# The stick-breaking values' projection computed token-major, with the activations stationary

## What is computed

```python
h = rms_norm(x, norm_mix_g[l])
proj = h @ w_in[l]
hq, hf, hi, hg, su, sq, sk, sv, gates = jnp.split(proj, split_at, axis=-1)
o_a = hgrn2_mixer(hq, hf, hi, hg, lb_all[l], hg_norm_g[l])
o_b = s5_mixer(su, ...)
o_c = stick_breaking_mixer(sq, sk, sv, sb_q_g[l], sb_k_g[l])
gate = jax.nn.sigmoid(gates)
merged = sum of gate_b * (o_b @ w_branch[b]) over the three branches
x = x + merged @ w_out[l]
x = x + gated_mlp(rms_norm(x))       # w_up, causal conv of width 3, silu, w_down
```

## Time and profile before

| | us |
|---|---|
| runs shown: median (lowest, highest) | 1436.39 (1435.6, 1438.55) |
| the profiled execution's own time | 1439.06 |
| its span, first to last instruction | 1437.3 |

### The profile page before, as it was taken

The page is one execution under the profiler, slowest core; times in us unless marked ns, Lnnn a source line. Parts: engine busy times, 40 slices in busy tenths (PEclk is TensorE's granted clock), DMA queues, the critical chain, the costliest instruction groups (busy, mean ns, idle before and its releaser), DMA issues.

```text
span 1437.3 us, 26837 instructions
## 1 busy us (share of the span) xinstructions
PE 1413.6 (98%) x9368; PEld 1294.8 (90%) x9368; DVE 1047.8 (73%) x1406; ACT 762.2 (53%) x1059; POOL 152.3 (11%) x195
## 2 busy tenths in 40 slices
PE   8979999999999999999999999999999999999999
PEld 7869998989999999988888888888888888888887
DVE  7897888688788757777687777777777776545443
ACT  6564678944433455454565555555555554344342
POOL 3210000000000002322111111111111110000000
PEclk9999999999999999999999999999999999999999
DMA  7544454445555556666656566656555666666663
GB/s 265 165 147 153 141 176 156 140 144 176 178 173 174 179 168 232 199 196 190 190 177 201 181 193 187 196 179 192 189 191 186 192 188 183 199 198 196 195 203 111
DMA packets 74346, 261.58 MB, mean 182 GB/s; under 512 B 8560, under 2 KB 9104, under 8 KB 74160
## 3 DMA queue, kind: packets, MB, share of 16 engines
q1 hardware_dynamic: 73152, 256.41, 56.6%
q0 software_dynamic: 992, 4.37, 0.9%
q10 hardware_dynamic: 144, 0.01, 0.0%
HBM read 258.66 MB, written 2.10 MB: 181 GB/s over the span
## 4 chain that ended last, share of the span: by engine, by line
PE 84%; DVE 7%; issue 3%; ACT 3%; POOL 1%; DMA 1%; POOLq 0%; SPq 0%; DVEq 0%; ACTq 0%
PE bank L325 38%; PE bank L339 22%; PE bank L327 20%; PE pair L371 3%; DVE w_lo L945 2%; ACT w_hi L642 1%; POOL merged L1496 1%; DMA raw<-w_br 1%; DVE tmp L953 1%; POOL merged L1498 1%; DVE a_in L1110 1%; DVE x_first L1106 0%; DVE tmp L960 0%; ACT tmp L652 0%; ACT a_raw L784 0%
## 5 line engine op out<-in xcount | busy, mean ns | idle before, releaser
L945 DVE TENSOR_TENSOR w_lo<-raw,w_hi 128x1024 fp32r<-128x1024 f32 (+1 forms) x499 | 590.9, 1193 | 323.2 <-ACT w_hi L642 318.7
L642 ACT ACTIVATE w_hi<-raw 128x1024 fp32r<-128x1024 f32 (+1 forms) x499 | 511.3, 1030 | 436.5 <-PE bank L327 221.4
L325 PE MATMUL bank<-h,w_hi 128*128 128x512 f32 x1408 | 488.4, 390 | 0.0
L327 PE MATMUL bank<-h,w_lo 128*128 128x256 f32 x1408 | 397.1, 282 | 0.0
L339 PE MATMUL bank<-a_in,w_hi 128*128 128x256 f32 x2048 | 364.7, 281 | 0.0
L339 PEld LDWEIGHTS bank<-a_in,w_hi 128*128 128x128 f32 x2048 | 314.2, 189 | 4.6 <-issue 4.6
L325 PEld LDWEIGHTS bank<-h,w_hi 128*128 128x128 f32 x1408 | 264.4, 188 | 55.4
L339 PE MATMUL bank<-a_in,w_lo 128*128 128x256 f32 x1024 | 286.9, 280 | 0.0
L327 PEld LDWEIGHTS bank<-h,w_lo 128*128 128x128 f32 x1408 | 266.1, 189 | 0.0
L325 PE MATMUL bank<-act,w_hi 128*128 128x512 f32 x704 | 244.1, 390 | 0.0
L327 PE MATMUL bank<-act,w_lo 128*128 128x256 f32 x704 | 198.5, 282 | 0.0
(11 more groups left out here) (188 smaller groups left out, 1299.9 us busy)
## 6 DMA issues: line engine op xcount, KB each, us to landing
raw<-w_up SPq DMA_DIRECT2D x176, 512.0 KB, 3.8
raw<-w_in SPq DMA_DIRECT2D x160, 512.0 KB, 4.2
raw<-w_down SPq DMA_DIRECT2D x80, 512.0 KB, 4.4
raw<-w_out SPq DMA_DIRECT2D x32, 512.0 KB, 4.2
raw<-w_br SPq DMA_DIRECT2D x16, 512.0 KB, 3.6
raw<-w_br SPq DMA_DIRECT2D x16, 256.0 KB, 3.3
raw<-w_down SPq DMA_DIRECT2D x16, 256.0 KB, 2.7
x_first<-xT SPq DMA_DIRECT2D x4, 512.0 KB, 7.2
```

The lines of the kernel that those rows point to most:

```text
L325: pe.matmul(bank[b][:, :], w[:, k * P:(k + 1) * P], a.rearrange("p a t -> p (a t)"), start=first and n == 0, stop=False, skip_group_check= ...
L327: mm = pe.matmul(bank[b][:, 0:SEQ], l[:, k * P:(k + 1) * P], a[:, 0, :], start=False, stop=last and n == len(blocks) - 1, skip_group_check ...
L642: act_e.activation(w_hi[s][:, 0:blocks * P], raw[s][:, 0:blocks * P], ACT.Copy).then_inc(hi_ready, 1)
L945: ve.tensor_tensor(w_lo[s][:, w], raw[s][:, w], w_hi[s][:, w].bitcast(F32), ALU.subtract).then_inc(lo_ready, 1)
```

## The change

The four SB value tiles (28 to 31, pieces 56 to 63) are computed token-major. `v_piece(q)` takes two blocks of features per piece; the activations of 128 tokens are stationary, and the weights of all four heads move, 512 columns in one matmul. Tokens 0 to 127 are summed in `bank[0]`, tokens 128 to 255 in `bank[1]`, over all eight pieces. SP loads each of these pieces as four runs of 256 columns of four tiles' pieces (1 KB each per partition). ScalarE leaves out `out_tile` of tiles 28 to 31; in step 31, after `hi` of pieces 66 and 67, it copies the two banks (`out_v`, 128x512 each) into the buffer of HGRN2's q. The array begins tile 32 when the first of these copies is done, tile 33 when the second is. The transposes `sb_vT` and the copy of their pair are gone; the rough root of k keeps its place. `out_count` translates tile numbers into the new count of `tile_out`.

```diff
+V_T = 7 * CT
...
+        def out_count(n):
+
+            return n - NORM_T + 1 if n < V_T + 2 else n - NORM_T - 1
+
...
-            with sp.Fori(HEAD_PIECES // RING, GLU_P // RING) as i:
+            with sp.Fori(HEAD_PIECES // RING, 2 * V_T // RING) as i:
+                for c in range(RING):
+                    load(i * RING + c, c, w_in[i * RING + c])
+            for q in range(2 * CT):
+                sp.wait_ge(lo_ready, 2 * V_T + q - (RING - 1))
+                cols = slice(2 * (q % CT) * P, 2 * (q % CT + 1) * P)
+                sp.dma_start(raw[q % RING].rearrange("p (c x) -> p c x", c=CT),
+                             w_in[2 * V_T + q // CT:2 * (V_T + CT):2, :, cols].rearrange("c p x -> p c x")).then_inc(raw_landed[q % RING], 16)
+            with sp.Fori(2 * (V_T + CT) // RING, GLU_P // RING) as i:
...
+            def v_piece(q):
+
+                p = 2 * V_T + q
+                pe.wait_ge(lo_ready, p + 1)
+                w, l = (x[p % RING].rearrange("p (c k j) -> p c k j", c=CT, k=2) for x in (w_hi, w_lo))
+                for i in range(2):
+                    k = 2 * q + i
+                    for t in range(2):
+                        rows = slice(t * P, (t + 1) * P)
+                        for m, (x, part) in enumerate(((w, 0), (l, 0), (w, 1))):
+                            mm = pe.matmul(bank[t][:, :].rearrange("p (c j) -> p c j", c=CT), a_in[:, k, part, rows], x[:, :, i, :],
+                                           start=k == 0 and m == 0, stop=k == KT - 1 and m == 2, skip_group_check=True)
+                return mm
...
-                if n == AT["sb_vT"]:
-                    group_ready(pe, SB_V)
-                    transposes("sb_vT", [group(SB_V)[:, h, b * P:(b + 1) * P] for b in range(2) for h in range(HEADS)])
...
-                    wait_taken(pe, "sb_vT")
+                    pe.wait_ge(tile_out, out_count(V_T + 1))
...
-                else:
-                    pe.wait_ge(tile_out, n - BANKS - NORM_T + 1)
+                elif n == V_T:
+                    pe.wait_ge(tile_out, out_count(V_T - 3))
+                elif not V_T < n < V_T + CT:
+                    pe.wait_ge(tile_out, out_count({V_T + CT: V_T, V_T + CT + 1: V_T + 1}[n] if n in (V_T + CT, V_T + CT + 1) else n - BANKS))
                 for h in range(2):
-                    in_piece(n, h).then_inc(piece_used, 1)
+                    if V_T <= n < V_T + CT:
+                        v_piece(2 * (n - V_T) + h).then_inc(piece_used, 1)
+                    else:
+                        in_piece(n, h).then_inc(piece_used, 1)
...
+            def out_v():
+
+                act_e.wait_ge(S("hg_factors"), 2 * LEVELS)
+                act_e.wait_ge(piece_used, 2 * (V_T + CT))
+                for t in range(2):
+                    act_e.activation(flat(HG_QQ)[:, t * 512:(t + 1) * 512], bank[t][:, :], ACT.Copy).then_inc(tile_out, 1)
...
-                if n == AT["sb_vT"] + 1:
+                if n == AT["k_ss"] + 2:
                     rough_root("k", T[6], T[5])
-                    wait_product(act_e, "sb_vT")
-                    taken(act_e.activation(flat(HG_QQ), product("sb_vT")[:, :], ACT.Copy), "sb_vT")
...
-                else:
+                elif not V_T <= n < V_T + CT:
                     out_tile(n)
+                elif n == V_T + CT - 1:
+                    out_v()
```

More of the change, by code:

```diff
@@ L87 @@
 assert all(x % RING == 0 for x in (GLU_P, BR_P, OUT_P, UP_P, DOWN_P, GLU_T, BR_T, OUT_T, UP_T, DOWN_T))
-AT = {"norm1": 6, "s5_bT": 9, "hg_vT": 14, "hg_o": 29, "hg_ss": 30, "q_ss": 34, "k_ss": 34, "sb_vT": 35,
+AT = {"norm1": 6, "s5_bT": 9, "hg_vT": 14, "hg_o": 29, "hg_ss": 30, "q_ss": 34, "k_ss": 34,
       "z0": 38, "z1": 38, "within0": 41, "within1": 41, "sb_o": 44}
@@ L94 @@
 AT.update({f"s5_y{c}": 48 + 8 * c for c in range(4)})
-KINDS = (["norm1", "s5_bT"] + [f"lev{k}" for k in range(LEVELS + 1)] + ["hg_vT", "hg_o", "hg_ss", "q_ss", "k_ss", "sb_vT"]
+KINDS = (["norm1", "s5_bT"] + [f"lev{k}" for k in range(LEVELS + 1)] + ["hg_vT", "hg_o", "hg_ss", "q_ss", "k_ss"]
          + ["z0", "within0", "z1", "within1", "sb_o"] + [f"bu{k}" for k in range(8)] + [f"s5_y{c}" for c in range(4)])
@@ L243, in group_ready @@
             else:
-                eng.wait_ge(tile_out, CT * (g + 1) - NORM_T)
+                eng.wait_ge(tile_out, out_count(CT * (g + 1) - 1))
         def wait_product(eng, name):
@@ L533, in _ @@
                     if 2 * m + i < BANKS:
-                        pe.wait_ge(tile_out, IN_TILES - NORM_T - BANKS + 2 * m + i + 1)
+                        pe.wait_ge(tile_out, out_count(IN_TILES - BANKS + 2 * m + i))
                     else:
@@ L1329, in gate_product @@
                     .then_inc(tile_summed, 1)
-            ve.wait_ge(tile_out, IN_TILES - NORM_T)
+            ve.wait_ge(tile_out, out_count(IN_TILES - 1))
             def branches(i, last):
```

## The result

| kernel | median of its runs, us | ratio to before, 95% interval |
|---|---|---|
| before | 1437.05 (11 runs) | |
| changed | 1441.67 (11 runs) | 1.0030 [1.0022, 1.0039] |
| changed, second series | 1440.58 (9 runs), before beside it 1436.78 | 1.0024 [1.0014, 1.0034] |

The change makes the kernel slower by 0.3%: 4.3 us (3.2 to 5.6) in the first series, 3.4 (2.0 to 4.9) in the second. One of the eleven changed executions of the first series took 6570.85 us and is left out of the ratio; the ten others have a median of 1441.2. The forecast was +2.9, 1439.3, in a range of 1435.8 to 1443.0. It was added to a median of 1436.39 from three executions; the eleven have 1437.05, so 0.7 us of the distance to 1441.67 is the base.

A forecast was written before the change was run, and what follows sets the result against it. The matrix array was taken as the bound (busy 98% of the span, 84% of the chain). Stall +2.4, transposes -1.0 and half clock +1.55 gave +2.9 us, 1439.3 on the median of 1436.39, range 1435.8 to 1443.0.

The forecast's parts named there:

- The new wait: Array before tile 32 waits for ScalarE's copy of bank 0: about 2.5 us idle, tile 32 begins 2.4 later.
- The lead of 0.17: ScalarE before tile 32: the array is 0.17 us early, so the split of piece 66 starts at 227.43 instead of 227.60.
- V matmuls: Tiles 28 to 31: 96 matmuls of 512 columns at 230 ns instead of 192 of 256, 0.3 us gained.
- Transposes: Eight value transposes and their copy out vanish ahead of the z products: -1.0 us together.
- the extra 0.1: Gap before the z products: without the copy the keys' norm comes 1.03 earlier, the array 0.87, another -0.1 us.
- The clock: Behind the new idle at tile 32 the array runs 3.4 us at half clock: +1.55 us, bounds 0 and 3.1.
- Nothing given back: Later array waits, 1.0 us for q's squares and 2.2 before 298.2, move with the array and absorb none of the stall.
- Sum: Whole kernel: +2.4 stall including the V matmuls' 0.3, -1.0 transposes, +1.55 clock, together +2.9 us.
- Rival 1: At tile 32 the full clock holds over the new idle: +1.4 us, 1437.8, within 0.2%; chance 0.20.
- Rival 2: The new stall shortens the 6.8 us of half clock after the wait before 298.2: 1436.2 to 1437.8; chance 0.14.
- Rivals 3 and 4: V tiles: slow 1 KB-row loads stall the array, 1445.8, chance 0.07; four-run moving operand is dearer, 1441 to 1450, chance 0.04.
- The 0.05 for faster by over 0.2%: Whole kernel: rival 2 together with rival 1 and a stall at its lower bound makes it faster; chance 0.05.

The follow-up runs named there:

- the other banks: Changed kernel with the V tiles summed in banks 2 and 3 and the first token half ahead within a piece; run twice: ratios 1.0001 and 1.0006 against before.
- the stall filled: Changed kernel with 11 matmuls of 128 columns on constants between the last V matmul and tile 32's wait: ratio 1.0017 against before.
- the wait alone: Kernel before with one edit, tile 32 waiting until tile 31 is copied out instead of tile 28: ratio 1.0032, +4.6 us.
- plain loads: Kernel with V tiles in banks 2 and 3, its eight V pieces loaded in rows of 4 KB: ratio 0.9993 against before.
- the moving operand in one run: Kernel with V tiles in banks 2 and 3 and 4 KB rows, moving weights as one run of 512 columns: matmuls 233 ns apart, single execution.

## Why the prediction was right, step by step

- **The new wait**: right in place, releaser and order (2.38 idle, inside 2.3 to 2.8). Tile 32 began 2.51 later instead of 2.4. The lead of 0.17, worked out from shorter V matmuls, wasn't there: from the first V matmul the split of piece 66 came 26.85 later (201.17 to 228.02), where before it came 26.87 later (200.73 to 227.60). The copy began 1.91 after that split and took 0.58 to 0.59, both as forecast.
- **V matmuls**: the term that was mis-sized most. Forecast 230 ns and 0.3 us gained, measured 233 ns and 0.02 us (26.86 in the other banks against 26.88). It hardly changed the sum, since ScalarE and not the last V matmul sets the start of tile 32; the idle before it was shorter for that (2.38 for 2.5). What it did move is the lead named above. I took the 512's distance from a pair of 512 and 256 in the up-projection; the three 256s of this very stage gave 233 for 512 columns, and that was the row to take. In this form a column costs the same in both, and the change gains nothing here.
- **Transposes**: -0.91 measured (q's squares to z: 26.30 against 27.21), forecast -1.0. The gap at the keys' norm is 0.20 against 0.22, so the extra 0.1 wasn't there.
- **The clock**: 3.4 us at 0.50 behind the stall, worth 1.55 (45.98 against 44.43 from tile 32 to z with the stall filled), both as forecast. A term was missing: the restart. The third matmul of tile 32 begins 0.34 behind the first (230.56 to 230.90) where 0.23 is usual: 0.1. It isn't the clock's: with the stall filled it is 0.34 as well (230.49 to 230.83).
- **Nothing given back**: right. The waits of 1.0 and 2.2 stand as they were, and with the wait alone the z products come 2.44 later, the 2.32 of the stall and the 0.1 of the restart.
- **Sum**: +2.95 forecast, +3.27 between the matmul starts (2.51 + 1.55 + 0.11 - 0.91 = 3.26); in time +4.3 and +3.4. The forecast in time was 0.5 to 1.4 too low. Of that the matmul starts account for 0.3; the rest is within the intervals, and no single profile fixes the mean clock that goes into it.
- **Rival 1** (full clock over the stall, once called the second in the prediction) didn't occur in either profile of the changed kernel, but did in the run with the wait alone, after 2.15 idle. So it is real, and the point from which it decides isn't an idle time between 1.0 and 2.2 as I wrote: the same idle is followed by either. **Rival 2** was at work (3.4 instead of 6.8 us behind the wait at 300 in the profile after) and is chance, as the table shows. **Rivals 3 and 4** fell.
- **The chances**: I put 0.49 on no difference and 0.46 on slower, with the sum on the line between them, 0.2%. The first series lies over that line, the second's interval (0.14 to 0.34%) on both sides of it, so of the two the runs favour the one that I gave slightly less. Three small terms (0.1 each: the start of tile 32, the restart, the norm) all erred to the cheap side. That the time still fell well inside the range owes something to the range's width of 7 us. The 0.05 for faster by over 0.2% doesn't follow from its own terms: the stall's lower bound of +1.5, -1.0 and -3.1 make -2.6, short of -2.9.

## What to carry to other kernels

When a projection sums several output tiles at once in the accumulators, the question is not what its matmuls cost but which bank the next tile needs, and where its copy stands in the queue of the engine that empties it. Choose banks that the following tiles don't need first, or move that copy ahead of other work: here either took back some 3 to 4 us, more than the 0.9 that the transposes save. A short stall costs more than its length on a kernel bound by the array, because the half clock may follow it.

## What the runs showed of the hardware

- The same wait of 2.2 us was followed by 0, 3.4 or 6.8 us at the half clock, in kernels that hardly differ around it. By this wait alone two executions can thus lie 3.1 us apart (estimate, 6.8 x 1.55/3.4), and a profile alone doesn't give the clock's share.
- Filling a stall of 2.4 us with products of constants went with the full clock behind it in both profiles that have it, where the changed kernel's two had 3.4 us at the half clock, and made the kernel 1.4 us (standard error 0.7) faster at the same start of the next tile.
- A 512-column float32r matmul stood 233 ns from the next where all are alike, and with one of 256 behind it the pair takes 346, against 350 for the same columns here; why the pair is cheaper stays open.
- Loads of 512 KB in rows of 1 KB landed after 3.3 to 5.3 us; in rows of 4 KB it was 3.2 to 5.2 before, 3.3 to 4.8 with plain loads and 3.3 to 5.3 with the moving operand in one run. No cost of the small rows shows.
